# Gate, branch and output products of a mixer in three fp32r passes, with a low part of each weight and input

## Chip, cores and metric

One core of a Trainium2 chip. The metric is the device time of one execution in microseconds (us), the median of the runs.

## What is computed

Two blocks of two layers each on 256 tokens of width 1024, all in fp32. The part in question is the first block's mixer, once per layer `l`:

```
h    = rmsnorm(x, norm_mix[l]) * (1 + sc_m) + sh_m
qa, ka, va, cq, ckv, kr, z, xbc, dt_raw, gates = split(h @ w_in[l])      # gates: 3 x 1024 columns
ya   = differential attention (qa, ka, va)                               # width 512
yb   = latent attention (cq, ckv, kr)                                    # width 512
yc   = rmsnorm(ssd(silu(conv(xbc)), dt) * silu(z))                       # width 1024
ga, gb, gc = split(sigmoid(gates))
x    = x + g_m * ((ga*(ya @ w_branch_a) + gb*(yb @ w_branch_b) + gc*(yc @ w_branch_c)) @ w_out)
```

Then comes a feed-forward with a short convolution. The second block has feed-forwards, a window attention and a convolution; the change doesn't touch it.

## The kernel before

Activations are kept transposed: 128 features on the partitions, 256 tokens along the free axis, so a width of 1024 is 8 pieces of 128x256. A weight is a row of 128x128 tiles. A *block* is the product that gives one piece of 128 output features: 8 tiles (contraction of 1024) for `gate`, `brC` and `out`, 4 tiles for `brA` and `brB` (contraction of 512). All weights stream from HBM in the order of use into `ring`, three slots of 24 tiles (1.5 MB each); SyncE fetches a slot when the semaphore `tiles_used` says that its tiles have been multiplied.

The feed-forwards split their operands already: ACT copies weights to fp32r (`w_hi`), DVE subtracts (`w_lo`), and TensorE (PE) adds high times high, high times low and low times high, in fp32r. In the mixers every product is fp32 from `ring` (L1152).

`mixer1` has two halves. The first makes the projections other than 16 gate blocks and does both attentions. The second follows a list of steps, `STEPS1B` (L157), written out by hand; every engine walks the same list in order (`steps_pe`, `steps_act`, `steps_dve`, and a loop on GpSimd, called POOL) and does what its own code has for the step, waiting on semaphores for the others:

```
silu; gate 8, gate 9; dt 0; xt 0; gate 10; xt 1; gate 11; xt 2, xt 3; gate 12; xt 4; dt 1;
cb 0; gate 13, 14; cb 1; gate 15; cb 2; gate 16; cb 3; decay 0; gate 17; decay 1; y 0; decay 2; gate 18, 19; y 1; ...
... y 5; gates 0; brA 0-3; y 6; brA 4-7; y 7; brB 0, 1; norm; gates 1; brB 2-7; brC 0-7; out 0-7
```

`silu` on ACT are eight 512-wide operations on xc (L1347), four on z, with table loads. `xt` and `dt` are PE transposes that ACT copies out (L1375, L1373); after `dt 1` POOL makes xw (L1583), which `cb 0` needs. `cb` are products of the state-space part, masked by DVE (L1498). `decay j`: PE spreads rows (L1259), DVE subtracts (L1511), ACT takes the exponential (L1385), DVE multiplies (L1520, L1524). `y j`: PE products (L1275 to L1279), DVE adds the skip term (L1529), POOL multiplies with z (L1591); behind every second y ACT squares (L882) and PE sums for the norm (L820). `gates 0` and `gates 1` are sigmoids on ACT with table loads. A projection block goes to `bank[i % 2]` and ACT copies it out (L1307); a branch block is multiplied with its gate by DVE (L1542 for brA, L1547 for brB and brC) and added by POOL (L1598); an `out` block is added to x by DVE (L1537), and ACT's square of it and a PE sum for the next norm follow (L397, L403).

Of the kernel before, what the change touches and what calls it, by code (L numbers as in the profile page):

```python
# [110 lines left out]
def steps1a(layer):  # L111
# [35 lines left out]
    else:  # L147
# [20 lines left out]
           + [("branch", b, j) for b in ("brC", "out") for j in range(8)])  # L168
WIDTH = {"uq": 2, "uk": 1, "uv": 1, "brA": 4, "brB": 4, "m0": 16, "m1": 16, "m2": 16, "n0": 16}
# [61 lines left out]
class Plan1:  # L231


    def __init__(self, layer):
        self.a = steps1a(layer)
        order = self.a + STEPS1B
# [42 lines left out]
NPARMAX = max(NPAR1, NPAR2)  # L279


def build(nc, A, out):
    ctx = ExitStack()
    with ctx:
# [5 lines left out]
        ring = sb("ring", [P, RING, SLOT])  # L290
# [4 lines left out]
        h = sb("h", [P, KD, T])  # L295
# [18 lines left out]
        def open_work():  # L314

            phase = ExitStack()
            phases["n"] += 1
            work["W"] = phase.enter_context(nc.sbuf_tensor(f"work{phases['n']}", [P, 119 * 256], F32))
            return phase
# [4 lines left out]
        def cut(n, shape=None):  # L324
            a = used["at"]
            used["at"] += n
            assert used["at"] <= 119 * 256, used["at"]
# [99 lines left out]
        def tile(t, base):  # L427

            return ring[:, (base + t // TPS) % RING, t % TPS * P:t % TPS * P + P]

# [394 lines left out]
        def mixer1(layer):  # L825
# [6 lines left out]
            krdt, z, xc = cut(T), cut(8 * T, (8, T)), cut(16 * T, (16, T))  # L832
            gates_at = used["at"]
            gates = cut(24 * T, (24, T))
            ya, yb = cut(4 * T, (4, T)), cut(4 * T, (4, T))
            lamc, tmp256 = cut(8), cut(T)
# [18 lines left out]
            ropet = cut(512)  # L855
# [65 lines left out]
            order = plan.a + STEPS1B  # L921
# [165 lines left out]

            def steps_pe(pe, steps):
                for step, kind, j in steps:
# [16 lines left out]
                    elif step in ("proj", "branch"):  # L1106
# [13 lines left out]
                        need(pe, seen, base, t0, t1)  # L1120
                        m_rows = P
# [13 lines left out]
                        elif kind == "brA":  # L1135
                            src = [ya[:, k, :] for k in range(4)]
                        elif kind == "brB":
                            src = [yb[:, k, :] for k in range(4)]
                        elif kind == "brC":
                            if j == 0:  # L1140
                                norm_ready(pe, ("ssm", 3))
                            src = [xc[:, k, :] for k in range(8)]
                        elif kind == "out":
                            src = [merged[:, k, :] for k in range(8)]
                        else:
                            src = [h[:, k, :] for k in range(8)]
                        for k, rhs in enumerate(src):
                            if step == "proj" and i == 0:
                                pe.wait_ge(S("m_h"), k + 1)
                            if kind == "out" and j == 0:  # L1150
# [1052 lines left out]
```

## Time and profile before

| | |
|---|---|
| median of 3 runs | 2521.34 us (2517.33 to 2521.93) |
| profiled execution | 2522.0 us, its span 2520.1 us |
| PE busy | 2358.9 us, 94% of the span |
| DVE busy | 1469.4 us, 58% |
| ACT busy | 1031.2 us, 41% |
| POOL busy | 52.6 us, 2% |
| mean granted clock of TensorE | 0.963 |
| HBM | 387.80 MB read, 154 GB/s over the span |

The span is the time from the first to the last instruction of one profiled execution. Busy time is the time in which at least one instruction of an engine runs. The granted clock is 1.00 at 2.4 GHz and 0.50 at 1.2 GHz. The second half of `mixer1` lies at 329.0 to 520.9 us in layer 0 and at 995.6 to 1187.5 us in layer 1.

### The profile page before, as it was taken

How to read it: one execution, taken by the hardware profiler on the slowest of the kernel's cores; microseconds unless marked ns; L12 is line 12 of the kernel's file. 1: busy time of each engine (PE TensorE's matmuls, PEld its weight loads, DVE VectorE, ACT ScalarE, POOL GpSimd, SP SyncE). 2: the span in 40 equal slices, each digit the busy share in tenths (PEclk: the TensorE clock that was granted, in tenths of full speed). 3: DMA queues.
4: the chain of work that ended last, by engine and by line, in shares of the span. 5: the costliest groups of instructions: out<-in, count | busy, mean ns of one | idle time of the engine just before them, and what ended most of it. 6: DMA issues, size and time to landing. Idle time of an engine off the chain costs nothing. (4 is left out here: it accounts for less than half of the span.)

```text
span 2520.1 us, 36502 instructions
## 1 busy us (share of the span) xinstructions
PE 2358.9 (94%) x13590; PEld 1997.1 (79%) x13590; DVE 1469.4 (58%) x2785; ACT 1031.2 (41%) x1824; POOL 52.6 (2%) x73
## 2 busy tenths in 40 slices
PE   6989988999999999989999999988999999978998
PEld 3656776889976677778999899856998899856997
DVE  4796605167643563232766766763766766763765
ACT  2222333145533334231555554434554554434554
POOL 0000000100000000011000000000000000000000
PEclk8999999999999999999999999979999999979999
DMA  8754222444545522224455455212554455213552
GB/s 312 258 209 166 101 101 75 151 150 180 193 153 215 211 101 101 101 101 152 176 186 188 168 191 189 95 51 100 202 198 150 151 200 189 94 43 112 199 189 92
DMA packets 37535, 390.11 MB, mean 155 GB/s; under 512 B 4416, under 2 KB 5056, under 8 KB 5952
## 3 DMA queue, kind: packets, MB, share of 16 engines
q1 hardware_dynamic: 37440, 388.87, 41.8%
q8 instruction: 56, 0.92, 0.1%
q14 instruction: 39, 0.32, 0.0%
HBM read 387.80 MB, written 1.05 MB: 154 GB/s over the span
## 5 line engine op out<-in xcount | busy, mean ns | idle before, releaser
L1152 PE MATMUL bank<-h,ring 128*128 128x256 f32 x2048 | 479.2, 390 | 13.1 <-ACT h L988 8.1
L1152 PEld LDWEIGHTS bank<-h,ring 128*128 128x128 f32 x2048 | 390.8, 194 | 104.6 <-issue 27.9
L633 DVE TENSOR_TENSOR ffn_w_lo<-ring,ffn_w_hi 128x2048 fp32r<-128x2048 f32 x126 | 288.8, 2292 | 165.6 <-ACT ffn_w_hi L582 165.5
L503 PE MATMUL bank<-ffn_hh,ffn_w_hi 128*128 128x512 f32 x1408 | 362.6, 399 | 13.1 <-DVE ffn_hh L763 9.0
L503 PEld LDWEIGHTS bank<-ffn_hh,ffn_w_hi 128*128 128x128 f32 x1408 | 257.2, 191 | 66.4 <-issue 9.2
L555 PE MATMUL bank<-ffn_g_hi,ffn_w_hi 128*128 128x256 f32 x1056 | 299.4, 284 | 6.2 <-DVE ffn_g_lo L678 6.1
L555 PE MATMUL bank<-ffn_g_lo,ffn_w_hi 128*128 128x256 f32 x1056 | 298.8, 283 | 0.0
L555 PE MATMUL bank<-ffn_g_hi,ffn_w_lo 128*128 128x256 f32 x1056 | 298.8, 283 | 0.0
L582 ACT ACTIVATE ffn_w_hi<-ring 128x2048 fp32r<-128x2048 f32 x126 | 240.0, 1905 | 0.8
L555 PEld LDWEIGHTS bank<-ffn_g_hi,ffn_w_hi 128*128 128x128 f32 x1056 | 202.7, 192 | 7.5 <-issue 7.4
L1152 PE MATMUL bank<-work,ring 128*128 128x256 f32 (+1 forms) x880 | 202.4, 385 | 0.4 <-DVE work L1547 0.4
L555 PEld LDWEIGHTS bank<-ffn_g_hi,ffn_w_lo 128*128 128x128 f32 x1056 | 202.7, 192 | 0.0
L555 PEld LDWEIGHTS bank<-ffn_g_lo,ffn_w_hi 128*128 128x128 f32 x1056 | 202.7, 192 | 0.0
L510 PEld LDWEIGHTS bank<-ffn_hh,ffn_w_lo 128*128 128x128 f32 x1408 | 191.5, 190 | 13.5
L1307 ACT ACTIVATE work<-bank 128x256 f32<-128x256 f32 (+2 forms) x168 | 63.8, 381 | 330.2 <-PE bank L1152 325.5
L1152 PEld LDWEIGHTS bank<-work,ring 128*128 128x128 f32 (+1 forms) x880 | 166.1, 190 | 39.5 <-issue 10.1
L493 PE MATMUL bank<-ffn_hh,ffn_w_hi 128*128 128x256 f32 x1408 | 188.9, 288 | 9.0 <-ACT ffn_hh L728 9.0
L510 PE MATMUL bank<-ffn_hh,ffn_w_lo 128*128 128x256 f32 x1408 | 195.7, 282 | 0.0
L493 PEld LDWEIGHTS bank<-ffn_hh,ffn_w_hi 128*128 128x128 f32 x1408 | 179.2, 195 | 11.2 <-issue 9.8
L638 DVE TENSOR_TENSOR ffn_w_lo<-ring,ffn_w_hi 128x1024 fp32r<-128x1024 f32 x132 | 160.8, 1218 | 3.4 <-ACT ffn_w_hi L595 3.4
L607 ACT ACTIVATE ffn_cv<-bank 128x256 f32<-128x256 f32 x176 | 57.8, 380 | 201.4 <-PE bank L510 201.4
L595 ACT ACTIVATE ffn_w_hi<-ring 128x1024 fp32r<-128x1024 f32 x132 | 137.6, 1043 | 0.0
(252 smaller groups left out, 2879.5 us busy)
## 6 DMA issues: line engine op xcount, KB each, us to landing
ring<-w_in SPq DMA_DIRECT2D x244, 1536.0 KB, 6.4
x<-x_in SPq DMA_DIRECT2D x1, 1024.0 KB, 15.4
mem<-mem_in SPq DMA_DIRECT2D x1, 1024.0 KB, 4.7
y_out<-x SPq DMA_DIRECT2D x4, 256.0 KB, 2.5
con<-con_in SPq DMA_DIRECT2D x1, 801.0 KB, 7.1
par<-par_in SPq DMA_DIRECT2D x2, 302.0 KB, 15.7
work<-pos_in SPq DMA_DIRECT2D x2, 128.0 KB, 6.0
par<-par_in SPq DMA_DIRECT2D x2, 76.0 KB, 5.4
```

Source lines behind the costliest of these rows:

```text
L493: m = pe.matmul(up_out(j, half, True), w_[:, j % 2, c0:c0 + P], hh[:, k, part, :], start=start and k == 0, stop=stop and k == KD - 1, skip ...
L503: pe.matmul(up_out(j, half, False), w_hi[:, j % 2, c0:c0 + P], hh[:, k, :, :], start=k == 0, stop=False)
L510: m = pe.matmul(up_out(j, half, False)[:, 0:T], w_lo[:, j % 2, c0:c0 + P], hh[:, k, 0, :], start=False, stop=k == KD - 1)
L555: mm = pe.matmul(acc[m_ // 2][:, m_ % 2 * T:m_ % 2 * T + T], w_[:, j % 2, c0:c0 + P], g_[:, j % 2, :], start=first and m_ % 2 == 0 and p_ ...
L582: act.activation(w_hi[:, j % 2, UP], ring[:, slot, UP], ACT.Copy).then_inc(S(tag + "_up_hi"), 1)
L595: act.activation(w_hi[:, j % 2, DOWN], ring[:, slot, DOWN], ACT.Copy).then_inc(S(tag + "_down_hi"), 1)
L607: act.activation(cv[:, j % 2, half, :], up_out(j, half, conv)[:, T:2 * T], ACT.Copy).then_inc(S(tag + "_part"), 1)
L633: dve.tensor_tensor(w_lo[:, j % 2, UP], ring[:, (base + j) % RING, UP], w_hi[:, j % 2, UP], ALU.subtract).then_inc(S(tag + "_up_lo"), 1)
L638: dve.tensor_tensor(w_lo[:, j % 2, DOWN], ring[:, (base + j) % RING, DOWN], w_hi[:, j % 2, DOWN], ALU.subtract).then_inc(S(tag + "_down_lo ...
L1152: m = pe.matmul(ps[0:m_rows, 0:T], tile(t0 + k, base)[:, 0:m_rows], rhs, start=k == 0, stop=k == len(src) - 1 and kind != "uk")
L1307: act.activation(dst[0:m_rows, :], bank[i % 2][0:m_rows, 0:T], ACT.Copy).then_inc(S("pj_free"), 1)
```

## The change

The 16 gate blocks of the second half and all branch and output blocks become three passes in fp32r: high weights times the high input, high weights times the low input, low weights times the high input, where high is a value copied to fp32r and low the difference. The blocks are taken in 40 *units* of 8 tiles (two brA or brB blocks, or one block of another kind). A new step `wsplit n` makes the parts of unit n: POOL copies the high weights of gate units, ACT those of the others, into one of two buffers (`AHEAD` = 2); DVE writes the low weights over the weights in `ring`. The step stands right behind the last block of unit n-2 (the first two behind `silu`), and the copy waits until PE has finished unit n-2.

Inputs are split too: h in the step `silu` (ACT ahead of the silus, DVE beside them), ya and yb in `ysplit` behind `cb 3`, the gated and normed xc in four `xsplit` steps (behind y 2, y 4, y 6 and brB 3), merged in eight `msplit` steps, each behind the brC block that comes one later. `out 0` goes tile by tile through its three passes, every other block pass by pass. ACT's table load behind the sigmoids now follows both `gates` steps; the squares of x move from the end into the `out` steps. Some small buffers share memory. The number and order of tiles and of transfers stay.

```diff
+AHEAD = 2
+def with_splits(steps, units):
+    early = {0: ("silu", "", 0), 1: ("silu", "", 0)}
+    after = {early[u]: [] for u in early}
+    for u in range(len(units)):
+        at = early[u] if u < AHEAD else ("proj" if units[u - AHEAD][-1][0] == "gate" else "branch", *units[u - AHEAD][-1])
+        after[at] = after.get(at, []) + [("wsplit", "", u)]
+    for at, step in [(("cb", "", 3), ("ysplit", "", 0)), (("y", "", 2), ("xsplit", "", 0)), (("y", "", 4), ("xsplit", "", 1)),
+                     (("y", "", 6), ("xsplit", "", 2)), (("branch", "brB", 3), ("xsplit", "", 3))] \
+            + [(("branch", "brC", min(k + 1, KD - 1)), ("msplit", "", k)) for k in range(KD)]:
+        after[at] = after.get(at, []) + [step]
+    return [s for step in steps for s in [step] + after.get(step, [])]
...
+            by_pool = lambda n: units[n][0][0] == "gate"
...
+            def weights_free(eng, n):
+                if n >= AHEAD:
+                    eng.wait_ge(S("tiles_used"), USED1[units[n - AHEAD][-1]][0])
+            def weights_low(dve, n):
+                for i, (g, c0, cols, at) in enumerate(pieces(unit_tiles[n], base)):
+                    dve.wait_ge(high_sem(n), high_count(n) + i + 1)
+                    dve.tensor_tensor(ring_low[:, g % RING, c0:c0 + cols], ring[:, g % RING, c0:c0 + cols],
+                                      w_high[:, n % AHEAD, at:at + cols], ALU.subtract).then_inc(S("w_low"), 1)
+            def split_product(pe, b, ps, high, low):
+                n, (t0, t1) = unit_of[b], TILES1[b]
+                first = b in (("out", 0), ("gate", 8))
+                pe.wait_ge(high_sem(n), high_count(n) + made(n))
+                if b == ("brA", 0):
+                    pe.wait_ge(S("y_low"), 2)
+                if b == ("brC", 0):
+                    pe.wait_ge(S("xc_low"), 4)
+                wide = range(t1 - t0)
+                order = [(p_, k) for p_ in range(3) for k in wide] if b != ("out", 0) else \
+                    [(p_, k) for k in wide for p_ in range(3)]
+                waited = False
+                for i, (p_, k) in enumerate(order):
+                    if p_ == 2 and not waited:
+                        pe.wait_ge(S("w_low"), low_count(n) + made(n))
+                        waited = True
+                    if first and p_ < 2:
+                        name = ("m_" if b[0] == "out" else "h_") + ("low" if p_ else "high")
+                        pe.wait_ge(S(name), k + 1)
+                    c0 = (t0 + k - unit_tiles[n][0]) * P
+                    g, r0 = (base + (t0 + k) // TPS) % RING, (t0 + k) % TPS * P
+                    w_ = ring_low[:, g, r0:r0 + P] if p_ == 2 else w_high[:, n % AHEAD, c0:c0 + P]
+                    m = pe.matmul(ps, w_, (low if p_ == 1 else high)[:, k, :], start=i == 0, stop=i == len(order) - 1)
+                m.then_inc(S("tiles_used"), USED1[b][1])
...
+            def square_of_x(act, j):
+                act.wait_ge(S("br_free"), br_index["out", j] + 1)
+                act.activation(h[:, j, :], x[:, j, :], ACT.Square).then_inc(S("b_next_squares"), 1)
...
+                    elif step == "wsplit" and not by_pool(j):
+                        weights_free(act, j)
+                        for g, c0, cols, at in pieces(unit_tiles[j], base):
+                            act.wait_ge(full[g % RING], 16 * (g // RING + 1))
+                            act.activation(w_high[:, j % AHEAD, at:at + cols], ring[:, g % RING, c0:c0 + cols],
+                                           ACT.Copy).then_inc(high_sem(j), 1)
+                    elif step == "ysplit":
+                        for n, src in enumerate((ya, yb)):
+                            act.activation(flat(y_high[:, 4 * n:4 * n + 4, :]), flat(src),
+                                           ACT.Copy).then_inc(S("y_high"), 1)
+                    elif step == "xsplit":
+                        norm_ready(act, ("ssm", j))
+                        act.activation(flat(xc_high[:, 2 * j:2 * j + 2, :]), flat(xc[:, 2 * j:2 * j + 2, :]),
+                                       ACT.Copy).then_inc(S("xc_high"), 1)
+                    elif step == "msplit":
+                        act.wait_ge(S("merged"), KD + j + 1)
+                        act.activation(merged_high[:, j, :], merged[:, j, :], ACT.Copy).then_inc(S("m_high"), 1)
                     elif step == "silu":
+                        for k in range(KD):
+                            act.activation(merged_high[:, k, :], h[:, k, :], ACT.Copy).then_inc(S("h_high"), 1)
...
-                        if j == 0:
-                            act.preload_act_table_set("natural_log_exp_and_others")
+                        act.preload_act_table_set("natural_log_exp_and_others")
+                    elif step == "branch" and kind == "out" and j:
+                        square_of_x(act, j - 1)
...
+                    elif step == "wsplit":
+                        weights_low(dve, j)
+                    elif step == "silu":
+                        for k in range(KD):
+                            dve.wait_ge(S("h_high"), k + 1)
+                            dve.tensor_tensor(h_low[:, k, :], h[:, k, :], merged_high[:, k, :],
+                                              ALU.subtract).then_inc(S("h_low"), 1)
+                    elif step == "msplit":
+                        dve.wait_ge(S("m_high"), j + 1)
+                        dve.tensor_tensor(merged_low[:, j, :], merged[:, j, :], merged_high[:, j, :],
+                                          ALU.subtract).then_inc(S("m_low"), 1)
...
+                    for step, kind, j in plan.b:
+                        if step == "dt" and j == 1:
+                            pool.wait_ge(S("tp_free"), TSEQ["dt", "", 1] + 1)
...
+                        if step == "wsplit" and by_pool(j):
+                            weights_free(pool, j)
+                            for g, c0, cols, at in pieces(unit_tiles[j], base):
+                                pool.wait_ge(full[g % RING], 16 * (g // RING + 1))
+                                pool.tensor_copy(w_high[:, j % AHEAD, at:at + cols],
+                                                 ring[:, g % RING, c0:c0 + cols]).then_inc(high_sem(j), 1)
```

## Rows read from the trace of the kernel before

**Rows 1.** Windows of mixer 1's second half: stretch, length, busy time (count) by engine, clock, DMA.

```profile
329.00:355.70 26.70, 20.85 (x105) 17.54 (x105) 2.81 (x8) 15.24 (x29) 1.90 (x1) 1.00 0.34 119
355.70:374.90 19.20, 19.16 (x88) 16.53 (x88) 1.77 (x8) 2.69 (x7) 0.00 (x0) 0.91 0.23 83
374.90:393.80 18.90, 17.92 (x92) 14.06 (x92) 10.09 (x37) 5.36 (x12) 1.45 (x2) 1.00 0.24 85
393.80:419.60 25.80, 24.82 (x130) 19.47 (x129) 15.11 (x49) 7.61 (x18) 2.17 (x3) 0.93 0.17 62
419.60:437.10 17.50, 11.64 (x41) 9.24 (x40) 6.57 (x19) 8.60 (x15) 0.73 (x1) 0.80 0.24 90
437.10:461.20 24.10, 23.92 (x124) 20.41 (x124) 7.99 (x19) 6.28 (x9) 6.42 (x9) 1.00 0.36 132
461.20:520.90 59.70, 59.53 (x275) 51.75 (x273) 7.66 (x17) 3.33 (x8) 6.63 (x10) 1.00 0.38 135
...
1127.80:1187.50 59.70, 58.99 (x273) 51.26 (x271) 7.66 (x17) 3.33 (x8) 6.54 (x10) 1.00 0.44 161
```

**Rows 2.** Groups by line: busy us, mean ns of one; idle before, and its releaser.

```profile
L1152 PE MATMUL bank<-h,ring 128*128 128x256 f32 x2048 | 479.2, 390 | 13.1 <-ACT h L988 8.1 <-ACT work L1307 3.4 <-PEq L927 1.6
...
L638 DVE TENSOR_TENSOR ffn_w_lo<-ring,ffn_w_hi 128x1024 fp32r<-128x1024 f32 x132 | 160.8, 1218 | 3.4 <-ACT ffn_w_hi L595 3.4
...
L595 ACT ACTIVATE ffn_w_hi<-ring 128x1024 fp32r<-128x1024 f32 x132 | 137.6, 1043 | 0.0
...
L752 POOL CAST ffn_w_hi<-ring 128x1024 fp32r<-128x1024 f32 x12 | 12.7, 1090 | 783.4 <-POOLq L707 393.9 <-POOLq L1658 327.9 <-POOLq L1560 61.6
```

**Rows 3.** Timeline (start us, us, what): DVE during brC, PE in a feed-forward.

```profile
482.51 0.42 DVE L1547 TENSOR_TENSOR work<-work,bank 128x256 f32<-128x256 f32 x1 [3.03 <-PE bank L1152]
...
485.96 0.42 DVE L1547 TENSOR_TENSOR work<-work,bank 128x256 f32<-128x256 f32 x1 [3.03 <-PE bank L1152]
...
583.24 0.28 PE L555 MATMUL bank<-ffn_g_hi,ffn_w_hi 128*128 128x256 f32 x1
...
586.00 0.28 PE L555 MATMUL bank<-ffn_g_hi,ffn_w_lo 128*128 128x256 f32 x1
```

**Rows 4.** Timeline of the second half's start: ACT and PE.

```profile
330.28 4.27 ACT L1347 ACTIVATE work<-work 128x512 f32<-128x512 f32 x8
...
338.37 3.72 PE L1152 MATMUL bank<-h,ring 128*128 128x256 f32 x16 [1.76 <-ACT work L1307]
```

**Rows 5.** Timeline from y 2 to y 4.

```profile
399.30 0.43 PE L1275 MATMUL bank<-work 128*64 128x128 f32 x2
...
406.26 0.48 DVE L1529 SCALAR_TENSOR_TENSOR work<-work,par,bank 128x256 f32<-128x256 f32 x1 [1.36 <-PE bank L1279]
...
406.82 0.72 POOL L1591 TENSOR_TENSOR work<-work 128x256 f32<-128x256 f32 x1 [5.05 <-DVE work L1529]
...
407.58 0.63 ACT L882 ACTIVATE work<-work 128x512 f32<-128x512 f32 x1 [2.01 <-POOL work L1591]
...
409.14 1.14 DVE L1520 SCALAR_TENSOR_TENSOR work<-work 128x128 f32<-128x128 f32 x4 [0.70 <-ACT work L1385]
...
412.77 0.43 PE L1275 MATMUL bank<-work 128*64 128x128 f32 x2
```

**Rows 6.** Timeline: DVE at the first decay, PE at the first norm sum.

```profile
376.08 1.12 DVE L1511 TENSOR_SCALAR work<-bank,work 128x128 f32<-128x128 f32 x4 [1.00 <-PE bank L1259]
...
393.10 1.13 PE L820 MATMUL bank<-work,ones 128*128 128x256 f32 x4 [0.98 <-ACT work L882]
```

**Rows 7.** Timeline of DVE under the casts of a feed-forward's first weights.

```profile
521.43 2.02 POOL L752 CAST ffn_w_hi<-ring 128x1024 fp32r<-128x1024 f32 x2 [30.79 <-POOLq L1560]
...
522.85 0.88 DVE L460 SCALAR_TENSOR_TENSOR h<-h,rs_x 128x256 f32<-128x256 f32 x1
523.76 0.42 DVE L461 SCALAR_TENSOR_TENSOR rs_x<-h,rs_x 128x256 f32<-128x256 f32 x1
```

**Rows 8.** Windows, a stretch of the second block's attention.

```profile
1670.80:1701.50 30.70, 24.38 (x65) 14.04 (x66) 21.23 (x67) 10.18 (x38) 0.00 (x0) 0.50 0.00 1
```

More of the change, by code:

```diff
@@ L168, with split_units @@
            + [("branch", b, j) for b in ("brC", "out") for j in range(8)])
+AHEAD = 2
+def split_units(steps):
+    units = []
+    for s in steps:
+        if s[0] == "branch" or s[0] == "proj":
+            if s[1] in ("brA", "brB") and s[2] % 2:
+                units[-1].append(s[1:])
+            else:
+                units.append([s[1:]])
+    return units
+def with_splits(steps, units):
[9 more added lines that the diff above has]
+    return [s for step in steps for s in [step] + after.get(step, [])]
 WIDTH = {"uq": 2, "uk": 1, "uv": 1, "brA": 4, "brB": 4, "m0": 16, "m1": 16, "m2": 16, "n0": 16}
@@ L429, in tile, with pieces @@
             return ring[:, (base + t // TPS) % RING, t % TPS * P:t % TPS * P + P]
+        def pieces(tiles, base):
+            out, t = [], tiles[0]
+            while t < tiles[1]:
+                end = min(tiles[1], (t // TPS + 1) * TPS)
+                out.append((base + t // TPS, t % TPS * P, (end - t) * P, (t - tiles[0]) * P))
+                t = end
+            return out
         def need(pe, seen, base, t0, t1):
@@ L1086, in norm_ready @@
                 eng.wait_ge(S("norm_done"), max(NSEQ[k] for k in keys) + 1)
+            units = plan.units
+            unit_of = {b: n for n, blocks in enumerate(units) for b in blocks}
+            unit_tiles = [(TILES1[blocks[0]][0], TILES1[blocks[-1]][1]) for blocks in units]
+            by_pool = lambda n: units[n][0][0] == "gate"
+            made = lambda n: len(pieces(unit_tiles[n], base))
+            high_count = lambda n: sum(made(m) for m in range(n) if by_pool(m) == by_pool(n))
+            low_count = lambda n: sum(made(m) for m in range(n))
@@ L1120, in steps_pe @@
                         need(pe, seen, base, t0, t1)
+                        if (kind, j) in unit_of:
+                            high, low = {"brA": lambda: (y_high[:, 0:4, :], y_low[:, 0:4, :]),
+                                         "brB": lambda: (y_high[:, 4:8, :], y_low[:, 4:8, :]),
+                                         "brC": lambda: (xc_high, xc_low),
+                                         "gate": lambda: (merged_high, h_low),
+                                         "out": lambda: (merged_high, merged_low)}[kind]()
+                            split_product(pe, (kind, j), ps[:, 0:T], high, low)
+                            if kind == "out" and j >= 2:
+                                next_sum(pe, "b", j - 2)
+                            continue
                         m_rows = P
```

107 lines of the change are left out of this document (67 added, 40 removed).

## Prediction

> **What bounds the kernel now.** I read the page's busy line and forty slices, then the matmul groups, then windows over the part the change touches, and there the timeline. The part touched is the second half of mixer 1, once per layer. Cut where its work changes, it takes 26.7, 19.2, 18.9, 25.8, 17.5, 24.1 and 59.7 us in layer 0, 191.9 in all; the same cuts moved by 666.6 us fit layer 1, whose last stretch is given too [rows 1]. The reader is to see three kinds of stretch. In the last two TensorE (PE) is busy for 99%, DVE for 13% to 33%, GpSimd (POOL) for 11% to 27%: nothing but fewer PE microseconds shortens them, and the helpers have room. In the two in the middle (374.9 to 419.6) PE is busy for 96% but DVE already for 56%, with steps that wait for one another. In the first (78% PE) and the fifth (67%) PE waits for ACT.
>
> **What a product costs.** One 128x128 tile against 256 columns in fp32 is two PE instructions (2048 of them with h [rows 2], for 64 blocks of 8 tiles in two layers); a block of 8 tiles comes every 3.45 us, as the gated products on DVE show (482.51, 485.96) [rows 3], so a tile takes 0.432 us. In fp32r an instruction starts every 0.120 us: the 24 of one feed-forward step start from 583.24 to 586.00, 23 gaps in 2.76 us [rows 3]. They alternate high and low weights as the new code does, each with its own weight load, so the price carries over. Three passes are 0.360 us: 0.072 saved a tile, 0.576 a block of 8 (2.88 instead of 3.456). A layer has 16x8 gate tiles, 32 + 32 for brA and brB, 64 + 64 for brC and out: 320 tiles, 23.0 us; for both layers 46 us if PE were the bound everywhere.
>
> **What it adds.** Per unit of 8 tiles (1024 columns): a high copy, 1.04 us on ACT for the 24 branch and output units or 1.09 on POOL for the 16 gate units, then a DVE subtraction of 1.22 [rows 2]. DVE gets 40x1.22 = 49 us a layer beside the 52 it has in these stretches [rows 1], and some 12 us for the low parts of h, y, xc and merged (0.42 per 256 columns, as its 256-wide products take now [rows 3]; wider ones at 1.22 per 1024). No new transfer, no new queue: SP issues the same slots on the same block ends. The high copy of unit n waits until PE has finished unit n-2, then the subtraction follows; both stand in program order, so DVE's older work queues behind a cast that PE's progress releases. That is the change's real cost, and it depends on the stage. I place the steps after one another from these rows, with 0.1 us for each hand-over between engines.
>
> Last stretch (brC, out; 59.7 us). A unit takes PE 2.88. Its successor but one has its high copy 1.15 after the unit's end and its low at 2.4, and it's needed at 2.88 (high) and 4.8 (third pass). DVE has 0.42 + 1.22 + 0.42 = 2.06 in 2.88, ACT 1.04 + 0.42. All hidden. 16 units save 9.2. At the seam, out 0 walks k by k and needs merged_low 6 and 7, which stand on DVE behind the product of brC 7 (0.5), the low of out 1 (to 2.4) and each other (2.9, 3.3), where PE wants the first at 2.3: a 0.7 stall. **-8.5.**
>
> Sixth (24.1): 4 brA and 8 brB blocks of 4 tiles save 12x0.288 = 3.5. But ACT's `gates 1` step with its table loads now stands ahead of the high copy for brB 6/7: about 1.1 to 1.3 us of stall (the step is near 4.8 us: four sigmoids at 4.27/8 each [rows 4], and of the fifth stretch's 5.9 of PE idle, which has eight of them, the rest is mostly table loads). **-2.2.**
>
> Fifth (17.5): PE waits for y 5's norm square, which ACT does after the sigmoids; a 1.04 high copy now stands ahead of those too. Four brA blocks give 1.15 back, the wait for y 5 to be handled by DVE costs nothing beside ACT's. **-0.3.**
>
> Fourth (25.8). Before, from y 2 to y 4 takes 412.77 - 399.30 = 13.47 us, of which 2x3.46 are gates [rows 5]. After, counted from the end of gate 20: cast to 1.15, low to 2.5, y 2 on DVE (0.48) to 3.0, the new xc_low to 3.7, the decay's four subtractions (1.12 [rows 6]) to 4.8, the exponential, four products (1.14) to 6.7, two more to 7.1 [rows 5]. PE meanwhile is through gate 21 at 5.1; its cast is ready at 6.3 but DVE makes that low from 7.1 to 8.3, then y 3 to 8.8; POOL's gating (0.72) to 9.6, ACT's square (0.63) to 10.3, the sum on PE to 11.1, gate 22 to 14.0. So the pair takes 14.0 instead of 13.5: two cheaper gates (1.15) are more than given back, since y 3 waits on DVE behind a low that PE doesn't need yet. Pairs without the xc_low and at the edges come out better; over the stretch I get 24.8. **-1.0.**
>
> Third (18.9). Between gate 16 and the first decay DVE now has a low (after its cast 2.3), the last cb product (0.5) and two y_low (2.4). Decay 0's subtractions, which now begin as soon as PE's rows are there (DVE has waited 1.00 for them), begin some 3 us later; PE waits 2.8 us before y 0, and the square behind y 1 makes it wait 3.0 where it waits 0.98 now [rows 6]. Three gates save 1.7. Result 21.8. **+2.9.**
>
> Second (19.2): four gates in PE-bound order; casts and lows are ready 1.3 us early or more. 4x0.576: **-2.3**, with the same dip of the clock (0.91 [rows 1]).
>
> First (26.7). Eight copies of h go ahead of the silus on ACT, whose eight 512-wide ones took 4.27 [rows 4]; at half that width about 0.3 each, 2.4 in all. Gate 10, which started at 338.37 when ACT had copied gate 8 out, starts 2.4 later. DVE's `dt` now waits behind the low of gate 11, which waits for gate 9's end: 3.0 us late at the second transpose. The two gates after it (1.15) bring the state product on POOL to be about 2 us late. **+2.0.**
>
> Sum: 2.0 - 2.3 + 2.9 - 1.0 - 0.3 - 2.2 - 8.5 = -9.4 us a layer.
>
> **Two costs that this schedule lacks.** POOL's cast against DVE: the L460 operation, two SBUF inputs, took 0.88 us under the cast of the feed-forward's first weights, and its neighbour L461 0.42 right after [rows 7]. So a cast holds such an operation for 0.45 to a cast's length. Of 16 casts a layer most meet an idle DVE (it is waiting for them); the one after gate 21 meets the decay products, its like recurs in some three rounds. Price: 0 to 4 us a layer; I take 1.0, near the 0.45 of the row. In the Trainium skill, "SBUF — State Buffer", section "Who interferes with whom", a VectorE instruction with two SBUF inputs contends with a GpSimd one that reads SBUF and the loser waits for the whole instruction; the trace agrees (0.88 for 0.42). By that rule alone each of the 16 casts could cost its full 1.09, some 17 us a layer, if each met a busy DVE on the path; by the row, about 1.
>
> The clock: the granted clock falls to 1.2 GHz for a few microseconds after PE has stood idle, 0.80 as the mean in the fifth stretch where ACT holds PE [rows 1]. The change opens new waits of 2.5 to 3 us in the first, third and fourth stretches. 0.91 over 19.2 us is some 3.4 us at half speed. A further stretch of that length costs at most 1.7. Bounds: nothing (they fall where PE waits anyway) and four of them, 6.8. I take one, 1.7.
>
> Then -9.4 + 1.0 + 1.7 = -6.7 a layer, -13.4 for both. The profiled execution has a span of 2520.1 and 2522.0 around it: span 2506.7, and taken from the median 2521.34, **2508**.
>
> **Rivals.** (a) The forecast: the branch products pay, the state-space part gives some back. 2500 to 2515; chance 0.56. (b) The middle hides its helpers better: if the third and fourth stretches keep their length less the gates' 7x0.576 = 4.0, the layer gains 9.4 + 1.9 + 4.0 = 15.3 less the two costs, 25 to 30 in all: 2491 to 2500. For it: DVE is idle for 44% there before. Against: its work stands in the order of PE's blocks, and a pair already counted comes to 14.0. Chance 0.15. (c) DVE and POOL get in each other's way up to the bound (4 instead of 1), plus another dip: 3.0 + 1.7 more a layer, -4 in all: 2515 to 2526, no clear change. Chance 0.19. (d) Slower: the clock stays down through the state-space part. In the second block's attention it was 0.50 for 30.7 us on end, with PE busy 24.4 of them [rows 8], so thin PE work can be held there. PE's work in the third and fourth stretches is 38.7 us at full clock (44.7 less 2 idle less 4.0) in 46.6; at half clock it would be 77, some 30 us a layer more. It decides from about four extra falls of 3.4 us a layer (6.8 against 6.7), and is slower by more than 5 us from six. Against: those stretches keep PE busy for 83%, with gates of 2.9 us between waits. Chance 0.10: 2526 and up.
>
> **How the numbers follow.** 0.2% is 5 us, what a measurement of this kernel can tell from no change. Faster means under 2516.3: all of (a) and (b), and a tenth of the rest: 0.74. Same, 2516.3 to 2526.4: most of (c): 0.15. Slower: (d) and the edge of (c): 0.11. The range takes (a), (b) down to 2493 and most of (c): 2493 to 2521.
>
> **What would show it.** Right: blocks of 2.9 us in brC, and 3.3 in out with its sum; last stretch near 51; the first late by 2; PE waits of about 3 us ahead of y 0 and the first norm sums, ended by DVE and ACT; subtractions of 1.22, a few stretched under casts. Wrong: a brC block above 3.0 (helpers late or the price not carried over), the middle shorter than before by 4 (b) or longer by over 8 (c, d), a granted clock under 0.8 there (d).

## The result, and the profile after

In 18 runs each the kernel after took 2524.06 us (2519.98 to 2529.90) and the kernel before 2520.58 (2515.82 to 2522.97): ratio 1.0018, 95% interval 1.0011 to 1.0025. It is slightly slower. The prediction was 2508, with a range of 2493 to 2521: both the sign and the range are wrong.

Page of the kernel after: the busy lines of PE, PEld, DVE, ACT and POOL, and the granted clock in 40 slices.

```profile
PE 2334.5 (92%) x14230; PEld 2005.7 (79%) x14230; DVE 1589.0 (63%) x2909; ACT 1097.2 (43%) x1916; POOL 91.3 (4%) x105
PEclk8999997999999999889999999978999999979999
```

PE is busy for 24.4 us less than before, and the span is 4.0 longer (2524.1). So the products did get cheaper, and PE waits more or runs slower somewhere. The slices, each 63.1 us long, show where: the seventh (379 to 442 us) has a clock of 0.7, the 17th and 18th (1010 to 1136) have 0.8. These are the middle of the second half in either layer. Windows of the kernel after, layer 0, cut at the same work as [rows 1] (columns as there: length, busy us and count of PE, PEld, DVE, ACT and POOL, clock, DMA share, GB/s):

```profile
329.80:361.30 31.50, 21.16 (x146) 18.96 (x146) 16.05 (x23) 17.92 (x37) 9.67 (x8) 0.94 0.27 101
361.30:377.70 16.40, 16.40 (x120) 15.82 (x120) 4.96 (x9) 2.69 (x7) 3.83 (x4) 0.91 0.26 97
377.70:403.60 25.90, 21.40 (x118) 18.18 (x117) 18.07 (x48) 7.55 (x15) 4.91 (x6) 0.77 0.17 61
403.60:429.60 26.00, 22.81 (x162) 20.21 (x160) 18.51 (x48) 8.54 (x19) 5.12 (x5) 0.90 0.17 61
429.60:446.90 17.30, 10.21 (x58) 9.22 (x56) 9.39 (x25) 10.90 (x17) 0.73 (x1) 0.70 0.25 91
446.90:471.60 24.70, 21.43 (x175) 20.22 (x175) 16.16 (x27) 13.51 (x17) 7.82 (x9) 1.00 0.35 129
471.60:521.40 49.80, 49.11 (x400) 47.78 (x399) 28.76 (x40) 21.03 (x31) 6.66 (x10) 1.00 0.44 163
```

Beside [rows 1], as predicted and as measured:

| stretch | first | second | third | fourth | fifth | sixth | last | sum |
|---|---|---|---|---|---|---|---|---|
| predicted, us | +2.0 | -2.3 | +2.9 | -1.0 | -0.3 | -2.2 | -8.5 | -9.4 |
| measured, us | +4.8 | -2.8 | +7.0 | +0.2 | -0.2 | +0.6 | -9.9 | -0.3 |
| clock, before to after | 1.00 to 0.94 | 0.91 to 0.91 | 1.00 to 0.77 | 0.93 to 0.90 | 0.80 to 0.70 | 1.00 to 1.00 | 1.00 to 1.00 | |

In layer 1 the second half has this window, 2.5 longer than before (190.3):

```profile
996.20:1189.00 192.80, 164.67 (x1167) 153.76 (x1167) 111.12 (x218) 81.72 (x141) 38.55 (x41) 0.88 0.30 111
```

The second and the last stretch, where PE is the bound, gain somewhat more than forecast. The others fall short of it: the first by 2.8, the third by 4.1, the fourth by 1.2 and the sixth by 2.8. Timeline of the kernel after in the first, third and sixth (start us, us, what, [idle before <- releaser]):

```profile
341.76 1.22 PE L1198 MATMUL bank<-merged_high,w_high 128*128 128x256 f32 x8 [1.80 <-ACT work L1420]
...
341.92 0.34 DVE L1635 TENSOR_SCALAR work<-work,par 16x256 f32<-16x256 f32 x1
...
344.88 1.52 DVE L1644 TENSOR_TENSOR_SCAN work<-ones,work 16x128 f32<-16x128 f32 x2
344.93 1.20 POOL L1754 CAST w_high<-ring 128x1024 fp32r<-128x1024 f32 x1 [4.30 <-PE bank L1198]
...
347.51 1.12 PE L1346 MATMUL bank<-con,work 128*128 128x128 f32 x4 [2.65 <-ACT work L1508]
...
348.28 2.06 PE L1198 MATMUL bank<-merged_high,w_high 128*128 128x256 f32 x8
...
379.61 2.35 DVE L1622 TENSOR_TENSOR y_low<-work,y_high 128x1024 fp32r<-128x1024 f32 x2
...
381.88 1.12 DVE L1665 TENSOR_SCALAR work<-bank,work 128x128 f32<-128x128 f32 x4
...
385.29 0.69 PE L1384 MATMUL bank<-work 128*64 128x128 f32 x2 [2.35 <-DVE work L1678]
...
389.25 2.08 PE L1198 MATMUL bank<-merged_high,w_high 128*128 128x256 f32 x8
...
402.06 2.07 PE L878 MATMUL bank<-work,ones 128*128 128x256 f32 x4 [2.15 <-ACT work L947]
...
463.87 1.28 ACT L1490 ACT_TABLE_LOAD   x1
465.16 1.06 ACT L1461 ACTIVATE w_high<-ring 128x1024 fp32r<-128x1024 f32 x1
...
466.25 1.23 DVE L1171 TENSOR_TENSOR ring_low<-ring,w_high 128x1024 fp32r<-128x1024 f32 x1 [2.95 <-ACT w_high L1461]
...
468.00 0.75 DVE L1701 TENSOR_TENSOR work<-work,bank 128x256 f32<-128x256 f32 x2
468.47 0.74 PE L1198 MATMUL bank<-y_high,w_high 128*128 128x256 f32 x4 [2.32 <-DVE work L1701]
...
474.46 0.42 DVE L1701 TENSOR_TENSOR work<-work,bank 128x256 f32<-128x256 f32 x1 [0.51 <-PE bank L1198]
```

Read four things there. (1) The waits that the prediction named are there and near its size: 2.65 before `xt 1` (at 347.51), 2.35 before y 0 (at 385.29; 2.8 predicted) and 2.15 before the first norm sum (3.0). (2) Behind each of them PE is at 1.2 GHz: eight fp32r tiles of gate 11 last 2.06 at 348.28 and of gate 18 2.08 at 389.25, where eight such tiles of gate 10 took 1.22 at 341.76, and the four products of the norm sum last 2.07, where [rows 6] has 1.13. (3) The `dt` arithmetic on DVE starts at 341.92, right behind a low part. (4) At 466 DVE has a low part whose cast ACT made only after its table load; the branch products that free PE's banks stand behind it, and PE waits 2.32.

### The profile page after: what moved, and what is told of

It reads as the page before. It is cut to its first block and busy times, and to the rows that moved or that the text cites. A ratio compares the mean times of both kernels' runs of the same rounds, so it can differ in the third digit from the quotient of the medians.

```text
span 2524.1 us, 38195 instructions
## 1 busy us (share of the span) xinstructions
PE 2334.5 (92%) x14230; PEld 2005.7 (79%) x14230; DVE 1589.0 (63%) x2909; ACT 1097.2 (43%) x1916; POOL 91.3 (4%) x105
## 5 line engine op out<-in xcount | busy, mean ns | idle before, releaser
L561 PE MATMUL bank<-ffn_hh,ffn_w_hi 128*128 128x512 f32 x1408 | 364.5, 400 | 13.4 <-DVE ffn_hh L821 9.4
L1263 PE MATMUL bank<-h,ring 128*128 128x256 f32 (+1 forms) x1536 | 358.1, 389 | 8.1 <-ACT h L1053 8.1
L1263 PEld LDWEIGHTS bank<-h,ring 128*128 128x128 f32 (+1 forms) x1536 | 291.3, 193 | 81.9 <-issue 23.2
L568 PEld LDWEIGHTS bank<-ffn_hh,ffn_w_lo 128*128 128x128 f32 x1408 | 191.6, 190 | 13.4
L1171 DVE TENSOR_TENSOR ring_low<-ring,w_high 128x1024 fp32r<-128x1024 f32 x80 | 98.7, 1236 | 95.1 <-POOL w_high L1754 57.9
L516 DVE SCALAR_TENSOR_TENSOR work<-bank,work 128x512 f32<-128x512 f32 (+2 forms) x52 | 31.6, 607 | 150.7 <-ACT work L964 124.0
```

The costliest lines, as they stand in the source:

```text
L561: pe.matmul(up_out(j, half, False), w_hi[:, j % 2, c0:c0 + P], hh[:, k, :, :], start=k == 0, stop=False)
L568: m = pe.matmul(up_out(j, half, False)[:, 0:T], w_lo[:, j % 2, c0:c0 + P], hh[:, k, 0, :], start=False, stop=k == KD - 1)
L1171: dve.tensor_tensor(ring_low[:, g % RING, c0:c0 + cols], ring[:, g % RING, c0:c0 + cols], w_high[:, n % AHEAD, at:at + cols], ALU.subtract ...
L1263: m = pe.matmul(ps[0:m_rows, 0:T], tile(t0 + k, base)[:, 0:m_rows], rhs, start=k == 0, stop=k == len(src) - 1 and kind != "uk")
```

## The experiments

All times below are medians of four to six runs against 11 or 12 of the kernel before on the same chip. The second half's length is taken from its first ACT instruction to just past the last output product.

### One part of the change alone

The branch and output products split, with the gates in fp32; and the gates split, with the others in fp32. `SPLIT` lists the blocks that are split. The parts of inputs that no split block needs are not made.

```diff
+    for u in range(len(full)):
+        if full[u][0] not in SPLIT:
+            continue
```

> The 24 branch and output units in three fp32r passes as in the change, the 16 gate blocks in fp32 as before (no split of h, no cast on POOL). Theory A (the gates' split is what costs: new waits in the state-space part and the half clock they bring): 12 to 18 us under before, near 2505, since y 7 to out 7 took 8.1 us less per layer in the changed kernel. Rival B (the branch part's own stalls at gates 1 and out 0 and its input splits eat it): within 5 us of before.

> The 16 gate blocks in three fp32r passes, branch and output products in fp32 as before. Theory A: the change minus the branches' gain, 2536 to 2542, with a granted clock of about 0.85 from cb 3 to y 6. Rival B (gates are neutral): 2518 to 2523.

Branches alone: 2512.08 us, ratio 0.9969 (0.9957 to 0.9981). Gates alone: 2533.39, ratio 1.0042 (1.0028 to 1.0055). The two add up: -8.9 and +12.5 give +3.6, and the whole change gave +3.5. Neither run reached what was expected of it (12 to 18 us less, and 2536 to 2542), but the signs are those expected. So the branch half pays, and the gate half costs 12 us though it saves PE 9.2 us a layer (128 tiles at 0.072).

### The clock held, in both kernels

Idle products, whose result nobody reads, go into PE's queue ahead of its waits, into a PSUM bank that is free then. After: 3 and 4 ahead of gates 8 and 10, 5 each ahead of xt 1, cb 0, y 0 and the first norm sum, 6 and 15 ahead of the next two, 4 ahead of brB 6. Before: 3 ahead of gate 10, 5 ahead of cb 0, 2, 2 and 13 ahead of the norm sums.

```diff
+            def keep_warm(pe, key, where):
+
+                for _ in range(FILL.get(key, 0)):
+                    pe.matmul(where[:, 0:T], ones[:, :], con[:, 0:T], start=True, stop=True, skip_group_check=True)
...
-                        pe.wait_ge(S("m_ready"), j + 1)
...
+                            keep_warm(pe, (step, kind, j), bank[6])
+                        pe.wait_ge(S("m_ready"), j + 1)
```

> The changed kernel with idle fp32 products (on constants, results never read) put ahead of PE's long waits in each layer: 3 before gate 8, 4 before gate 10, 5 before xt 1, cb 0, y 0 and the first norm sum, 6 and 15 before the next two, 4 before brB 6; each is 0.43 us at full clock. Theory C (the clock): the second half stood at half clock for some 78 us in both layers against some 29 before; the fills keep it up and the time falls by 10 to 20 us, to 2504 to 2514, with the waits about as long as now. Rival D (the clock is along for the ride, the chain over DVE, ACT and POOL sets the length): the granted clock rises but the time stays within 3 us of the changed kernel's 2524.

> Control: the kernel before with idle products ahead of its own long waits in each layer (3 before gate 10, 5 before cb 0, 2 before the first two norm sums, 13 before the third). Theory C (the clock), by its half-clock time of 13.7 us a layer: at most half of it comes back, 5 to 12 us in all, near 2512, less than the 23 us that the same means gave the changed kernel; so the change made the clock worse. If it gives some 20 us here too, the fills repair something that the change did not cause.

After, filled: 2501.24 us, 0.9919 (0.9906 to 0.9932). Before, filled: 2506.54, 0.9952 (0.9939 to 0.9965). The kernel before gains more than the 5 to 12 us expected: 14.9 by the medians, 10.6 between the spans of the profiled executions (2520.1 and 2509.5). Windows of layer 0's second half, cut at cb 0, at the first norm sum and at y 7. Kernel before (its first part, 26.70, stands in [rows 1]):

```profile
355.70:393.10 37.40, 36.38 (x177) 29.95 (x177) 11.69 (x44) 7.56 (x18) 1.45 (x2) 0.95 0.24 85
393.10:445.30 52.20, 45.36 (x217) 36.27 (x217) 24.02 (x74) 16.70 (x32) 3.63 (x5) 0.90 0.21 74
445.30:519.70 74.40, 74.22 (x351) 64.94 (x350) 13.48 (x31) 9.19 (x16) 12.32 (x17) 1.00 0.38 140
```

The same of the kernel before, filled:

```profile
329.00:355.80 26.80, 24.55 (x122) 20.46 (x122) 2.81 (x8) 15.25 (x29) 1.90 (x1) 1.00 0.33 118
355.80:391.40 35.60, 35.60 (x180) 29.40 (x180) 11.66 (x44) 7.57 (x18) 1.45 (x2) 1.00 0.25 90
391.40:439.90 48.50, 48.26 (x248) 38.75 (x247) 23.89 (x74) 16.70 (x32) 3.63 (x5) 1.00 0.22 81
439.90:514.30 74.40, 74.22 (x351) 64.92 (x350) 13.49 (x31) 9.19 (x16) 12.26 (x17) 1.00 0.37 139
```

The kernel after (its first part, 31.50, is shown above):

```profile
361.30:402.10 40.80, 36.30 (x233) 32.77 (x233) 21.99 (x53) 9.55 (x21) 8.73 (x9) 0.83 0.21 78
402.10:453.90 51.80, 41.51 (x280) 37.34 (x280) 33.89 (x83) 22.79 (x40) 6.96 (x7) 0.84 0.20 71
453.90:520.20 66.30, 62.52 (x511) 61.02 (x510) 39.98 (x59) 31.48 (x44) 13.36 (x17) 1.00 0.43 160
```

The kernel after, filled:

```profile
331.70:363.20 31.50, 28.29 (x179) 25.11 (x180) 15.98 (x23) 17.94 (x37) 9.65 (x8) 0.95 0.27 101
363.20:399.00 35.80, 35.12 (x252) 31.28 (x252) 21.92 (x53) 9.37 (x21) 9.58 (x9) 1.00 0.24 89
399.00:446.80 47.80, 45.97 (x322) 40.47 (x322) 33.87 (x83) 22.98 (x40) 7.09 (x7) 1.00 0.21 75
446.80:513.10 66.30, 64.24 (x519) 62.39 (x518) 39.99 (x59) 31.48 (x45) 13.37 (x17) 1.00 0.43 161
```

Each pair of tables shows what the falls of the clock cost, since the work is the same: before, 37.4 - 35.6 and 52.2 - 48.5, together 5.5; after, 40.8 - 35.8 and 51.8 - 47.8, together 9.0. Nothing is lost in the last part, nor in the first part before. Layer 1 gives 190.3 - 185.3 = 5.0 before and 192.8 - 181.3 = 11.5 after. Over both layers the change adds 20.5 - 10.4 = 10.1 us of clock, 5 a layer. The two filled tables side by side show what the schedule does with the clock up: +4.7, +0.2, -0.7, -8.1, in all -3.9 a layer, where the prediction had -8.4 (-9.4 with the 1.0 for POOL).

One part of this comparison is not clean. The first part of the kernel after is 31.5 long with idle products and without, but for two reasons that cancel. With them the clock there is still only 0.95: PE ran much of gates 8 and 9 at 1.2 GHz, and the low part ahead of `dt` and so `xt 1` came 1.5 later (19.2 behind the half's start instead of 17.7). From `xt 1` to `cb 0` it then took 12.3 instead of 13.8, with gate 11 at full clock. The kernel after, filled:

```profile
350.89 0.66 PE L1384 MATMUL bank<-con,work 128*128 128x128 f32 x4 [0.77 <-ACT work L1547]
351.31 1.19 PE L1212 MATMUL bank<-merged_high,w_high 128*128 128x256 f32 x8
```

So an estimate from both traces for a first part with the clock up all through is 17.7 + 12.3 = 30.0. By it the schedule has -5.4 a layer instead of -3.9, and the clock costs some 6.5 instead of 5.

### Low parts made late

DVE's low parts of a unit whose step stands behind a gate block are made just ahead of the next block's step; PE, ACT and POOL keep their order.

```diff
+        if s[0] == "wsplit" and steps[n - 1][0] == "proj" and steps[n - 1][2] in (8, 9, 10, 11, 12, 13, 14, 15, 16, 17, 18, 19, 20, 21, 22, 23):
+            held.append(s)
+            continue
+        if s[0] == "proj" or s[0] == "branch":
+            out += held
+            held = []
...
-            steps_dve(dve, Engine(dve, "dve"), plan.b)
+            steps_dve(dve, Engine(dve, "dve"), plan.d)
```

> The changed kernel with one thing moved: DVE makes the low weights of a unit whose step stands behind a gate block only just ahead of the next block's step, behind the cb, decay, y and norm work that stands between. Casts, copies and PE's order stay. Theory E (DVE's program order, a low that PE does not need yet ahead of y and decay): PE's waits before the norm sums fall from 2.5 to 3.6 us to about 1.5, the time by 4 to 8 us. Rival D' (PE's waits come from ACT and from the chain itself): within 3 us of 2524.

2511.28 us, ratio 0.9966 (0.9954 to 0.9979): 13 us less than the kernel after, from an order on DVE alone, and more than the 4 to 8 expected. `dt` now starts at 339.54, 10.1 us behind the half's start instead of 12.1, and the first part is 28.1 long instead of 31.5. `xt 1` comes 1.7 earlier. PE waits 0.89 before it instead of 2.65, gate 11 behind it runs at full clock, and to `cb 0` it takes 12.1 instead of 13.8. Timeline of DVE in this kernel:

```profile
338.28 1.23 DVE L1195 TENSOR_TENSOR ring_low<-ring,w_high 128x1024 fp32r<-128x1024 f32 x1 [2.13 <-POOL w_high L1792]
339.54 0.34 DVE L1673 TENSOR_SCALAR work<-work,par 16x256 f32<-16x256 f32 x1
...
343.52 0.73 DVE L1682 TENSOR_TENSOR_SCAN work<-ones,work 16x128 f32<-16x128 f32 x2
```

Its mean clock in the two second halves is 0.90 and 0.91, against 0.91 and 0.88. PE stands idle there for 22.7 and 24.1 us instead of 28.9 and 28.1: the waits are shorter. In layer 1 its busy time is 3.8 less too, at the better clock.

> Both repairs on the changed kernel: late lows on DVE, and idle products cut to the shorter waits that it leaves (3 before gate 8, 2 before xt 1, 5 before cb 0, 4 before y 0, 2, 4 and 15 before the norm sums, 4 before brB 6). If order and clock are separate costs: 13 + 23 less their overlap, 2490 to 2494. If the late lows only gained by shortening the time at half clock, no better than the filled kernel: 2499 to 2502.

Late low parts and idle products together: 2502.18 us, 0.9933 (0.9920 to 0.9945), the same as idle products alone (2501.24). The two edits are worth 13 and 23 us alone and 22 together. By the four parts of layer 0 this kernel has 28.1, 35.8, 50.1 and 66.3, with idle products alone 31.5, 35.8, 47.8 and 66.3. So the 3.4 gained ahead of cb 0 stays gained, and 2.3 of it is given back between the first norm sum and y 7, where the clock is 0.97 against 1.00. In layer 1 the half is 181.8 against 181.3.

```diff
-    for at, step in [(("cb", "", 3), ("ysplit", "", 0)), (("y", "", 2), ("xsplit", "", 0)), (("y", "", 4), ("xsplit", "", 1)),
+    for at, step in [(('decay', '', 2), ("ysplit", "", 0)), (("y", "", 2), ("xsplit", "", 0)), (("y", "", 4), ("xsplit", "", 1)),
```

> As the kernel with both repairs, and the split of ya and yb moved from behind cb 3 to behind decay 2, off the way to the first decay. If y_low's 2.35 us on DVE held the first decay: 2 to 4 us less than that kernel, 2487 to 2491. If ACT's y_high then delays an exponential instead: the same.

The kernel above with the copies and low parts of ya and yb moved from behind cb 3 to behind decay 2, where the prediction had put 2.4 us on the first decay: 2501.97 us, 0.9932 (0.9915 to 0.9949). No change against 2502.18: they are not what holds the half up once the low parts are late.

### Which products are worth splitting, with the clock held

`SPLIT` without the gates, and idle products in the same places: 3 ahead of gate 10, 5 of cb 0, 3 of y 0, 2, 2 and 15 of the norm sums, 4 of brB 6.

> Gates in fp32, branch and output products in three passes, with idle products ahead of the waits (3 before gate 10, 5 before cb 0, 3 before y 0, 2, 2 and 15 before the norm sums, 4 before brB 6). What the gates' split is worth once the clock is held: if it is worth most of its 18.4 us with late lows (7.1 to 18), this kernel is 7 us or more above the one with both repairs, 2498 to 2504; if the split is worth nothing even then, within 3 us of it.

2499.57 us, 0.9915 (0.9901 to 0.9930). Against the whole change with idle products (2501.24) the gates' split now costs some 1.7 us instead of 12 by the medians, within the runs' scatter. The profiled executions are 7.4 apart (spans 2496.7 and 2504.1): the second half is 177.8 in both layers, 7.5 less than in the filled kernel before, and with the gates split too it is 181.4.

```diff
-                        for n in range(8) if j == 0 else range(8, 12):
+                        for n in range(12) if j == 0 else range(0):
...
-                        act.preload_act_table_set("natural_log_exp_and_others")
+                        if j == 0:
+                            act.preload_act_table_set("natural_log_exp_and_others")
```

> The kernel with fp32 gates, split branches and idle products, and all twelve sigmoids in the step gates 0 (20 idle products there, none before brB 6); gates 1 is gone with its two table loads. PE then waits about 2.1 us longer for the third norm square, but the waits of 1.1 and 2.6 us in brB, which I put down to DVE's products queued behind a low weight whose high copy ACT makes after gates 1, go. If that is their cause: 1 to 2 us a layer under 2499.6, 2496 to 2498. If the waits stay, they come from the norm and its apply: 2503 or more.

All twelve sigmoids in `gates 0`, so that no table load stands ahead of brB's casts: 2498.37 us, 0.9909 (0.9894 to 0.9923). PE's waits in brB are 0.80 and 0.26, where the kernel after has 0.79 and 2.32, but the third norm sum came 2.2 later than in the kernel above, behind the four sigmoids. The half is 178.0: one wait was traded for another.

```diff
-    for at, step in [(("cb", "", 3), ("ysplit", "", 0)), (("y", "", 2), ("xsplit", "", 0)), (("y", "", 4), ("xsplit", "", 1)),
+    for at, step in [(('dt', '', 1), ("hsplit", "", 0)), (("cb", "", 3), ("ysplit", "", 0)), (("y", "", 2), ("xsplit", "", 0)), (("y", "", 4), ("xsplit", "", 1)),
...
-                first = b in (("out", 0), ("gate", 8))
+                first = b in (("out", 0), ("gate", 13))
```

> The same kernel with fp32 gates and idle products (2499.6), but gates 13 to 16, the stretch where PE had nothing to wait for, in three passes; h is split behind dt 1. If the split pays wherever PE is the bound and helpers are idle: 4 x 0.576 = 2.3 us a layer less, 2494 to 2496. If the split of h and the casts disturb the start of cb: no gain, 2499 or more.

Gates 13 to 16 split as well, those of the PE-bound second stretch, with h split behind `dt 1`: 2497.16 us, 0.9907 (0.9895 to 0.9920). The window of layer 0's second half of this kernel:

```profile
328.50:503.90 175.40, 170.12 (x1139) 151.72 (x1139) 98.14 (x206) 81.98 (x141) 25.72 (x29) 1.00 0.33 118
```

175.4 is 2.4 less than 177.8 with these four in fp32, near 4x0.576 = 2.3. Where PE is the bound, splitting a gate pays in full by the windows. The medians are 2.4 apart for both layers together, less than the 4.8 of the windows and within the runs' scatter.

> Both of these together: the sum of their gains, about 2492 to 2495, the best version if both theories hold; else no better than the better of the two.

The last two together: 2498.24 us, 0.9913 (0.9900 to 0.9926), second half 175.5. It adds nothing, where 2492 to 2495 was expected.

### The gates' casts on ACT

```diff
-            by_pool = lambda n: units[n][0][0] == "gate"
+            by_pool = lambda n: False
```

> The changed kernel, unfilled, with the high weights of the gate units copied by ACT instead of POOL. What the port costs: DVE's two-input operations are no longer stretched under a cast (L1674 in the fourth stretch 1.93 instead of 1.14, the scan at the start 1.52 instead of 0.73). But ACT makes 16 copies of 1.04 us more a layer, two of them ahead of the silus. If POOL's port is the larger cost: 2518 to 2522. If ACT's queue is: 2526 to 2532.

2546.75 us, ratio 1.0107 (1.0092 to 1.0122): 23 us slower than the kernel after, and slower than either expectation. The timeline shows why, PE ahead of gate 8 in this kernel:

```profile
342.32 2.05 PE L1211 MATMUL bank<-merged_high,w_high 128*128 128x256 f32 x8 [13.38 <-ACT w_high L1488]
```

The cast stands behind the copies of h and the silus in ACT's queue, and PE waits 13.38 us. cb 0 comes 43.2 after the start instead of 31.5. What POOL costs DVE is small beside that.

## Why the prediction was wrong

It forecast -6.7 a layer; the second halves came out at -0.3 and +2.5, +1.1 in the mean. The 7.8 us between are two terms of the sum: the clock by 3.3 and the schedule by 4.5 as the tables with idle products stand, or by 4.8 and 3.0 with the first part put right as above.

**The clock: the term that failed most clearly.** "I take one, 1.7", of bounds 0 to 6.8. The runs with idle products give 5 a layer (3.5 in layer 0, 6.5 in layer 1), and 6.5 by the estimate above. The mechanism and the places were named: new waits in the first, third and fourth stretches. What was mis-sized is how many of them bring a fall. Its own three places at up to 1.7 each would have been 5.1, near what was measured; it took one of them without a row that would tell the one that counts from the two that don't. In layer 0 PE ran at 1.2 GHz behind three waits before the change (ahead of cb 0, of the first and of the third norm sum) and behind six after it (`xt 1`, cb 0, y 0 and all three norm sums). Most of the cost is in the third stretch, 0.77 over 25.9 us against 1.00 over 18.9, since full-rate work stands right behind the wait there. Rival (d) had this mechanism with its threshold, "about four extra falls", and 0.10; its strong form, a clock that stays down at 0.50, did not come. The Trainium skill, "TensorE: Matmul & The Clock Gate", section "HAM oscillation — how this bites in real kernels", tells of a kernel that falls to the lower clock again in each of its waits and pays after each. The trace agrees in kind: 2.08 instead of 1.22 for the eight tiles at 389.25, behind a wait of 2.35.

**The schedule with the clock up: -3.9 measured, -8.4 forecast.** Cut as in the four-part tables, the steps had +2.0, +0.6, -2.5 and -9.5, and the runs gave +4.7, +0.2, -0.7 and -8.1, POOL's share among them. By part:

- First stretch, "+2.0": +4.7. The prediction had the second transpose, `xt 1`, late by 3.0 and reckoned that two cheaper gates would bring that to 2. `xt 1` is late by 4.3 (17.7 behind the half's start instead of 13.4): the way to it runs through `dt` behind a low part, DVE's arithmetic, ACT's exponentials and the scan, which a cast stretched (1.52 for two, 0.73 in the kernel with late low parts). From `xt 1` to cb 0 the two cheaper gates do give their 1.15 back where the clock is up (12.1 to 12.3 instead of 13.4), but in the kernel after gate 11 runs at 1.2 GHz behind the wait before `xt 1`, and it takes 13.8. So of the +4.7 some 3.2 is the schedule and 1.5 the clock, which falls for a wait that the schedule made. Taking the low part out of `dt`'s way gave back 3.4, about half of it ahead of `xt 1` and half behind it: shown by that run and its trace.
- Second and third: -2.3 and +2.9, +0.6 together; measured +0.2 with the clock up. Right. What four of these gates save is shown apart, 2.4. Without idle products the two stretches up to the first norm sum have +3.4 (40.8 against 37.4), and 3.2 of that is the clock.
- From the first norm sum to y 7: -0.7 with the clock up, where the steps give -2.5 (-1.0, -0.3, and 4x0.288 of brA). The norm sums of the two kernels with idle products place it (391.44, 404.91, 423.27 before and 399.03, 413.65, 432.00 after). From the first to the second it takes 14.6 instead of 13.5, from the second to the third 18.4 in both, from the third to y 7 14.8 instead of 16.6. The fourth stretch, forecast at -1.0, thus gains nothing: the first of its two pairs is 1.1 longer, where the prediction had 0.5, and the second no shorter. 0.75 of the 1.1 is a decay product under a cast (1.89 for four instead of 1.14), which the prediction had under POOL.
- brB: a stall of "1.1 to 1.3". It was 0.79 and 2.32. The high copy was late by ACT's table load, as forecast, but the stall is longer because DVE's queue is in order: the low part that waits for this copy stands ahead of the branch products that free PE's two banks, and those then stand behind a second subtraction, for xc. That the copy's lateness is what counts is shown by the run with all sigmoids in one step, where the second wait is 0.26. The prediction had asked what stands behind the late copy on ACT, and not on DVE.
- Last stretch, "-8.5": -9.9. Right in kind; a block is 2.83 (471.64, 474.46, 477.29) rather than 2.88, and the seam's stall was 0.5 rather than 0.7. The fourth part as a whole gains 8.1 instead of 9.5; about 1 of the 1.4 is brB's longer stall less these gains, and the rest was not taken apart.

**POOL against DVE, "1.0" of 0 to 4.** About right. Three of the 16 casts of layer 0 meet a two-input DVE operation on its way and hold it by some 0.8 each, and two of them, at the scan and at a decay product (1.93 for four, 1.14 in [rows 5]), stand ahead of something that PE waits for: 1.6, argued from the trace and not tried apart. POOL's own product ahead of cb 0 is held in turn while DVE makes a low part (2.11 at 359.07, 1.90 before). Here is the group of the casts and that of the subtractions in the kernel after (count | busy, mean ns | idle before, its releasers):

```profile
L1171 DVE TENSOR_TENSOR ring_low<-ring,w_high 128x1024 fp32r<-128x1024 f32 x80 | 98.7, 1236 | 95.1 <-POOL w_high L1754 57.9 <-ACT w_high L1461 37.1
...
L1754 POOL CAST w_high<-ring 128x1024 fp32r<-128x1024 f32 x32 | 33.9, 1063 | 702.2 <-POOLq L992 599.2 <-PE bank L1198 103.0
```

The subtraction has waited for the cast, so the two seldom meet. The rule that each cast costs its whole length, 17 us a layer, did not come true, and moving the casts to ACT made it 23 us worse. For the casts that do meet, the trace agrees with what the Trainium skill states in "SBUF — State Buffer", section "Who interferes with whom": a VectorE instruction with two SBUF inputs contends with a GpSimd instruction that reads SBUF.

**Chances.** By the prediction's own bounds 2524 is "same", which had 0.15, though the interval shows the 3.5 us more to be real; 0.11 stood on slower. The time lies in the range of (c), 0.19, but not by its cause: POOL against DVE costs some 1.6 and not 4, and more than one further dip came. (d) had the right cause, more falls, at a weaker dose. What came, some three falls more together with a middle part that DVE holds up, had no chance of its own. Rival (b), a middle that hides its helpers, is refuted: even with the clock up the two parts from cb 0 to y 7 gain 0.5 together, where (b) had 6.3 for the second to fourth stretch alone.

**Open.** The best kernel has second halves 15 us shorter than before, 30 in both layers, and gains 23.6. In its profiled execution the part behind layer 1's second half is 4.4 us longer than before (1338.7 against 1334.3) and the part between the two halves 1.6 longer; no run looked into that. Layer 1 of the kernel after is 2.4 longer than layer 0 with the same instructions. The trace shows where: up to cb 0 it loses 1.1, with the clock down at gates 8 and 9, and 1.2 each between the norm sums, where the falls last longer; from cb 0 to the first norm sum it is 1.3 shorter. Why the clock falls or stays down at one place in one layer and not in the other is open. The passes of gate 8 with the low weights, in layer 0 and in layer 1:

```profile
335.47 1.21 PE L1198 MATMUL bank<-merged_high,ring_low 128*128 128x256 f32 x8 [0.75 <-DVE ring_low L1171]
...
1001.86 2.08 PE L1198 MATMUL bank<-merged_high,ring_low 128*128 128x256 f32 x8 [0.55 <-DVE ring_low L1171]
```

## What to carry to other kernels

Where an engine waits inside a half-full stretch, cheaper matmuls shorten its busy time and not its path, and they add idle time that can cost the clock: count each new wait as a fall until a row shows otherwise, or put idle products ahead of the waits and measure the schedule by itself (here worth some 14 us before the change and 23 after it, the largest effect in this study). They can miss a fall, as at gates 8 and 9 here, so look at the clock of every part before calling it held. Split only where PE is the bound: the branch and output products and four of sixteen gates, with idle products, take 2497 us, 9 less than the kernel before with idle products alone and 24 less than without. When a helper is added to an in-order queue, ask of every instruction behind it who waits for that one, and place the helper by its due time: the order of DVE's low parts alone moved 13 us.

## What the runs showed of the hardware

- An fp32r tile of 128x128 against 256 columns costs 0.118 us in brC (a block of 24 instructions every 2.83), against 0.432 for the same tile in fp32, so three passes save 18% of PE's time.
- A DVE scan with two SBUF inputs, 16x128, is held by a POOL cast as a two-input product is: 1.52 for two against 0.73. The cast is stretched too (1.20 against 1.04).
- Behind gaps of 2.65 before `xt 1` and 2.35 before y 0 PE ran at 1.2 GHz in the kernel after; one of 1.80 before gate 10 left the eight tiles behind it at 1.22, full speed. The same place need not do the same twice: gate 8's third pass took 1.21 in layer 0 and 2.08 in layer 1, behind gaps of 0.75 and 0.55.
